# First attention of a two-block kernel: meta scores in one matmul per tile, norms of two units at once, five probability buffers and one unit more of lag

## What is computed

```python
def gqa_block(q_blk, k, v):
    s = jnp.einsum('bkgqd,bksd->bkgqs', q_blk, k).astype(jnp.float32) * (HEAD_DIM ** -0.5)
    p = jax.nn.softmax(s, axis=-1)
    return jnp.einsum('bkgqs,bksd->bkgqd', p.astype(v.dtype), v)
...
        a_out = attention_branch(q, k, v, q_g, k_g, cos, sin, n_tok) * jax.nn.silu(a_gate)
        mixed = jnp.concatenate([f_out, a_out], axis=-1)
        h = h + jnp.einsum('ble,ed->bld', mixed, w_out[i])
```

## Time and profile before

| | |
|---|---|
| median of 3 runs | 2139.82 us (2139.18 to 2145.11) |
| profiled execution | 2138.93 us, span of the instructions 2137.1 us |
| TensorE matmuls | busy 1979.6 us (93%) |
| TensorE weight loads | 1627.8 us (76%) |
| VectorE | 1333.7 us (62%) |
| ScalarE | 917.1 us (43%) |
| GpSimd | 929.2 us (43%) |
| mean granted TensorE clock | 0.973 |
| first attention | scores of unit 0 start at 307.4 us, last values matmul at 545.7 us |

### The profile page before, as it was taken

One profiled execution on the slowest core, in us unless ns is written; L12 is line 12 of the kernel. 1 busy time (PEld: TensorE's weight loads), 2 busy tenths in 40 slices (PEclk: granted clock), 3 DMA queues, 4 the chain that ended last, 5 costly groups with the idle time before them and its releaser, 6 DMA issues.

```text
span 2137.1 us, 25608 instructions
## 1 busy us (share of the span) xinstructions
PE 1979.6 (93%) x9543; PEld 1627.8 (76%) x9543; DVE 1333.7 (62%) x1860; ACT 917.1 (43%) x1614; POOL 929.2 (43%) x651
## 2 busy tenths in 40 slices
PE   5999999999999999997998798889999999999888
PEld 5987767777787888876777686767888887777776
DVE  5354058988786354455566546777655568868846
ACT  4112127878442223235666544543333343435541
POOL 0333308988000000005665100589999996746030
PEclk9999999999999999998999999999999999999999
DMA  3112100000323111100000221323232338676212
GB/s 149 50 40 90 50 0 1 1 1 1 138 91 137 48 40 40 40 22 30 21 20 21 107 90 60 138 89 119 89 109 81 117 108 307 226 264 209 79 40 99
DMA packets 68412, 179.57 MB, mean 84 GB/s; under 512 B 6529, under 2 KB 8321, under 8 KB 68289
## 3 DMA queue, kind: packets, MB, share of 16 engines
q1 hardware_dynamic: 44928, 124.39, 17.4%
q10 hardware_dynamic: 23360, 53.54, 7.0%
HBM read 148.02 MB, written 29.88 MB: 83 GB/s over the span
## 4 chain that ended last, share of the span: by engine, by line
PE 63%; DVE 15%; POOL 8%; issue 7%; ACT 5%; DMA 1%; ACTq 0%; SPq 0%; DVEq 0%; POOLq 0%
PE psb L341 14%; PE psa L341 12%; PE psc L2472 4%; PE psa L2472 4%; POOL wrf L2334 4%; PE psd L2472 3%; PE psb L2472 3%; PE psd L989 2%; PE psd L1925 2%; POOL wrl L2352 2%; PE psc L967 2%; PE psd L341 1%; DVE ltl L1909 1%; DVE wl L370 1%; PE psc L341 1%
## 5 line engine op out<-in xcount | busy, mean ns | idle before, releaser
L2334 POOL TENSOR_TENSOR wrf<-wr 128x512 f32<-128x512 f32 x155 | 250.2, 1618 | 245.2 <-DMA wr<-slabs 237.6
L1877 POOL TENSOR_TENSOR lps<-lps,tiny 128x128 f32<-128x128 f32 (+2 forms) x24 | 14.7, 615 | 454.6 <-DVE tiny L1872 452.0
L2347 ACT ACTIVATE wrh<-wrf 128x512 fp32r<-128x512 f32 x155 | 97.7, 630 | 180.0 <-POOL wrf L2334 178.0
L2352 POOL TENSOR_TENSOR wrl<-wrf,wrh 128x512 fp32r<-128x512 f32 x111 | 168.3, 1523 | 8.4 <-ACT wrh L2347 8.3
L1128 POOL TENSOR_TENSOR pb<-pb,tiny 128x1024 f32<-128x1024 f32 x64 | 121.3, 1896 | 79.0 <-DVE tiny L1087 77.4
L341 PE MATMUL psb<-mh,wh 128*128 128x512 f32 x352 | 125.0, 399 | 4.1 <-issue 2.4
L364 ACT ACTIVATE wh<-wraw 128x1024 fp32r<-128x1024 f32 x82 | 86.2, 1053 | 87.2 <-PE psb L341 45.9
L341 PE MATMUL psb<-ml,wh 128*128 128x512 f32 x352 | 123.1, 394 | 0.0
L341 PE MATMUL psb<-mh,wl 128*128 128x512 f32 x352 | 122.7, 393 | 0.0
L370 DVE TENSOR_TENSOR wl<-wraw,wh 128x1024 fp32r<-128x1024 f32 x75 | 92.1, 1231 | 35.3 <-ACT wh L364 31.4
L2352 POOL TENSOR_TENSOR wrl<-wr,wrh 128x512 fp32r<-128x512 f32 x62 | 106.7, 1724 | 16.3 <-ACT wrh L2347 15.9
(11 more groups left out here) (641 smaller groups left out, 5937.8 us busy)
## 6 DMA issues: line engine op xcount, KB each, us to landing
wraw<-slabs SPq DMA_DIRECT2D x98, 512.0 KB, 3.5
wr<-slabs SPq DMA_DIRECT2D x132, 256.0 KB, 4.6
wr<-slabs SPq DMA_DIRECT2D x40, 512.0 KB, 3.5
hidden<-hf ACTq DMA_DIRECT2D x22, 512.0 KB, 3.5
half_sums<-hsum ACTq DMA_DIRECT2D x22, 256.0 KB, 3.6
x<-xT SPq DMA_DIRECT2D x8, 520.0 KB, 9.5
h<-xT SPq DMA_DIRECT2D x8, 512.0 KB, 7.2
residual<-h ACTq DMA_DIRECT2D x8, 512.0 KB, 6.1
```

Of the source, the lines that this page charges most:

```text
L2334: e.tensor_tensor(WRF[n % NW][:, :], x, y, WEIGHTS[product(n)][2]).then_inc(*pooled.up(("sum", n)))
L2347: e.activation(WRH[n % NW][:, :], x, ACT.Copy).then_inc(*acted.up(("high part", n)))
L2352: e.tensor_tensor(WRL[n % NW][:, :], x, WRH[n % NW][:, :], SUB).then_inc(*pooled.up(("low", n)))
```

## The change

Five things, all in the first attention:

- The two parts of the keys lie in one tile KEYS, so one matmul per tile of queries reads the 16 meta columns of both parts, 32 columns. The two products lie side by side in PSUM. ScalarE copies the high one, and VectorE adds the low one to it (`dve_meta_scores`) before the maxima.
- The norms are made for two units at once, in every second step. The factor of 2 leaves the norm; a half is applied to the output instead, as a scale in ScalarE's copy and in VectorE's scalar-tensor-tensor.
- There are five probability buffers; exp of unit u waits for the transposes of unit u - 5.
- Transposes and their parts run 4 units behind the scores (LAG1), the values 8 (AHEAD).
- GpSimd's counter for the product of a unit is raised ahead of the meta product, which gets a counter of its own; the norms wait for that of an earlier unit.

```diff
-        KHH = [at(f"khh{j}", [P, L], F32R, 137.5 + 8.25 * j) for j in range(2)]
-        KLL = [at(f"kll{j}", [P, L], F32R, 141.625 + 8.25 * j) for j in range(2)]
+        KEYS = [at(f"keys{j}", [P, 2, 1056], F32R, 137.5 + 8.25 * j) for j in range(2)]
+        KHH = [k[:, 0, 0:L] for k in KEYS]
+        KLL = [k[:, 1, 0:L] for k in KEYS]
...
-        PB = [at(f"pb{j}", [P, T], F32, (154.75, 158.75, 112.75, 116.75)[j]) for j in range(4)]
+        PB = [at(f"pb{j}", [P, T], F32, (154.75, 158.75, 112.75, 116.75, 107.25)[j]) for j in range(5)]
...
-        LAG, AHEAD = 3, 7
+        LAG = 3
+        LAG1, AHEAD = 4, 8
...
-                o = PS[Dp][:, 0, v * META:v * META + META]
-                e.matmul(o, lhsT=QST[s][:, c0:c0 + P], rhs=KHH[s][:, T:L], start=True, stop=False,
-                         skip_group_check=True)
-                t = e.matmul(o, lhsT=QST[s][:, c0:c0 + P], rhs=KLL[s][:, T:L], start=False, stop=True,
+                t = e.matmul(PS[Dp][:, 0, 2 * v * META:2 * v * META + 2 * META].rearrange("p (a b) -> p a b", b=META),
+                             lhsT=QST[s][:, c0:c0 + P], rhs=KEYS[s][:, :, T:L], start=True, stop=True,
                              skip_group_check=True)
...
-                if 0 <= u - LAG < NU:
-                    pe_turns(e, u - LAG)
+                if 0 <= u - LAG1 < NU:
+                    pe_turns(e, u - LAG1)
...
-            if u >= 4:
-                e.wait_ge(*psum.on(("turned", u - 4, 1)))
-            e.activation(PB[v][:, :], both(u % 2), ACT.Exp, scale=scale1, bias=NB[:, v:v + 1],
+            if u >= 5:
+                e.wait_ge(*psum.on(("turned", u - 5, 1)))
+            e.activation(PB[u % 5][:, :], both(u % 2), ACT.Exp, scale=scale1, bias=NB[:, v:v + 1],
...
-        def dve_meta_max(e, g):
-            e.wait_ge(*acted.on(("meta s", g)))
-            e.tensor_reduce(MXT[:, 4 * (g % 2):4 * (g % 2) + 4], SMC[:, g % 2, :].rearrange("p (a b) -> p a b", b=META),
-                            AX.X, MAX).then_inc(*vec.up(("meta max", g)))
+        def dve_meta_scores(e, g):
+
+            e.wait_ge(*acted.on(("meta s high", g)))
+            e.tensor_tensor(meta_scores(g), meta_scores(g), meta_product(1), ADD).then_inc(*vec.up(("meta s", g)))
+            e.wait_ge(*vec.on(("meta s", g)))
+            e.tensor_reduce(MXT[:, 4 * (g % 2):4 * (g % 2) + 4], meta_scores(g), AX.X, MAX).then_inc(*vec.up(("meta max", g)))
...
-        def dve_norms(e, u):
-            v = u % 4
-            e.wait_ge(*acted.on(("exps", u)))
-            e.tensor_scalar(RI[:, v:v + 1], RSA[:, v:v + 1], RSM[:, v:v + 1], 2.0, ADD, MUL
-                            ).then_inc(*vec.up(("all sum", u)))
+        def dve_norms(e, u, n):
+
+            v = slice(u % 4, u % 4 + n)
+            e.wait_ge(*acted.on(("exps", u + n - 1)))
+            if u >= 4:
+                e.wait_ge(*pooled.on(("meta p", u + n - 5)))
+            e.tensor_tensor(RI[:, v], RSA[:, v], RSM[:, v], ADD).then_inc(*vec.up(("all sum", u)))
             e.wait_ge(*vec.on(("all sum", u)))
-            e.reciprocal(RI[:, v:v + 1], RI[:, v:v + 1]).then_inc(*vec.up(("one over", u)))
+            e.reciprocal(RI[:, v], RI[:, v]).then_inc(*vec.up(("one over", u + n - 1)))
...
-                if 0 < u - 1 < NU:
-                    dve_norms(e, u - 1)
+                if u == 2:
+                    dve_norms(e, 1, 1)
+                elif u > 2 and u % 2 == 0 and u <= NU:
+                    dve_norms(e, u - 2, 2)
...
-            e.tensor_tensor(OT[g % 2][mine, :], OT[g % 2][mine, :], PS[Dp][mine, 1, :], ADD
-                            ).then_inc(*vec.up(("out", g)))
+            e.scalar_tensor_tensor(out=OT[g % 2][mine, :], in0=PS[Dp][mine, 1, :], scalar=0.5, in1=OT[g % 2][mine, :],
+                                   op0=MUL, op1=ADD).then_inc(*vec.up(("out", g)))
```

More of the change, by code:

```diff
@@ L770, in fourier_free @@
             elif n == 7:
-                e.wait_ge(*acted.on(("meta s", 0)))
+                e.wait_ge(*vec.on(("meta s", 0)))
             elif n >= 2:
@@ L850, in dve_fourier @@
                 if n == 4:
-                    dve_meta_max(e, 0)
+                    dve_meta_scores(e, 0)
         def dve_four(e, n):
@@ L966, in pe_turns @@
                     c = (4 * h + kt) * P
-                    t = e.transpose(PS[C][:, h, kt * P:kt * P + P], PB[u % 4][:, c:c + P], SQC[:, 0, :])
+                    t = e.transpose(PS[C][:, h, kt * P:kt * P + P], PB[u % 5][:, c:c + P], SQC[:, 0, :])
                 t.then_inc(*psum.up(("turned", u, h)))
@@ L971, in pe_meta_turn @@
             e.wait_ge(*pooled.on(("meta parts", g)))
-            e.wait_ge(*acted.on(("meta s", min(g + 2, NG - 1))))
+            e.wait_ge(*vec.on(("meta s", min(g + 2, NG - 1))))
             for x in range(4):
@@ L1028, in act_parts, with meta_product, meta_scores @@
                              ).then_inc(*acted.up(("p high", u, h)))
+        def meta_product(part):
+            return PS[Dp][:, 0, 0:8 * META].rearrange("p (v a b) -> p v a b", a=2, b=META)[:, :, part, :]
+        def meta_scores(g):
+            return SMC[:, g % 2, :].rearrange("p (a b) -> p a b", b=META)
         def act_meta_scores(e, g):
@@ L1033, in act_meta_scores @@
                 e.wait_ge(*vec.on(("meta max", g - 2)))
-            e.activation(SMC[:, g % 2, :], PS[Dp][:, 0, 0:4 * META], ACT.Copy).then_inc(*acted.up(("meta s", g)))
+            e.activation(meta_scores(g), meta_product(0), ACT.Copy).then_inc(*acted.up(("meta s high", g)))
         def act_attention(e):
@@ L1038, in act_attention @@
                 g, phase = divmod(u - AHEAD, 4)
-                if 0 <= u - LAG < NU:
-                    act_parts(e, u - LAG)
+                if 0 <= u - LAG1 < NU:
+                    act_parts(e, u - LAG1)
                 if u < NU:
@@ L1057, in act_attention @@
                         e.wait_ge(*pooled.on(("gated", g - 2)))
-                    e.activation(OT[g % 2][mine, :], PS[Dp][rest, 1, :], ACT.Copy).then_inc(*acted.up(("out low", g)))
+                    e.activation(OT[g % 2][mine, :], PS[Dp][rest, 1, :], ACT.Copy, scale=0.5).then_inc(*acted.up(("out low", g)))
                 if u % 4 == 2 and u < NU - 4:
@@ L1117, in dve_attention @@
                 if u % 4 == 3 and u < NU - 4:
-                    dve_meta_max(e, u // 4 + 1)
-                if 0 <= u - LAG < NU:
-                    dve_parts(e, u - LAG)
+                    dve_meta_scores(e, u // 4 + 1)
+                if 0 <= u - LAG1 < NU:
+                    dve_parts(e, u - LAG1)
         def pool_attention(e):
@@ L1126, in pool_attention @@
                 if u < NU:
-                    e.wait_ge(*vec.on(("one over", u)))
-                    e.tensor_tensor(PB[v][:, :], PB[v][:, :], RI[:, v:v + 1].to_broadcast([P, T]), MUL)
+                    e.wait_ge(*vec.on(("one over", u if u < 2 else u // 2 * 2 + 1)))
+                    e.tensor_tensor(PB[u % 5][:, :], PB[u % 5][:, :], RI[:, v:v + 1].to_broadcast([P, T]), MUL
+                                    ).then_inc(*pooled.up(("p", u)))
                     e.tensor_tensor(PM[g % 2][:, v, :], PM[g % 2][:, v, :], RI[:, v:v + 1].to_broadcast([P, META]), MUL
-                                    ).then_inc(*pooled.up(("p", u)))
+                                    ).then_inc(*pooled.up(("meta p", u)))
                 if u < NU and v == 3:
@@ L1143, in pool_meta_parts @@
                 e.wait_ge(*psum.on(("meta turned", g - 2)))
-            e.wait_ge(*pooled.on(("p", 4 * g + 3)))
+            e.wait_ge(*pooled.on(("meta p", 4 * g + 3)))
             hi = PMS[g % 2][:, :, 0:META]
```

6 lines of the change are left out of this document (3 added, 3 removed).

## The result

The changed kernel takes 2146.37 us (median of 20 runs, 2141.84 to 2153.11), the kernel before 2139.65 (20 runs, 2134.23 to 2145.14). The ratio is 1.0034, with a 95% interval of 1.0026 to 1.0042: slower, by about the least that can be told apart. The time lies in the range on record, but 6 us above the forecast and not in the case held likeliest, no change, which had 0.76; slower had 0.11.

The account below looks back on a forecast made before the run. The prediction took a chain over ScalarE and VectorE to the output, plus GpSimd waits, to bound TensorE's loop. Terms 5.5 + 0.4 - 4.6 - 0.3 - 0.4 = +0.6 us gave 2140.4 us, range 2132 to 2147.

Parts of the forecast that it names:

- The meta matmuls at the new place: Loop, ahead of the light step: four meta matmuls lose their cover, +0.42 us per group, +5.5 us over 13 groups.
- GpSimd's waits: Loop: the lag makes GpSimd's products 2.2 us early, so all TensorE waits on GpSimd go, -4.6 us.
- The VectorE part: Loop, chain to the output: norm pair -0.04 us and output +0.07, together +0.03 per group, +0.4 us.
- The output: VectorE's output addition as scalar-tensor-tensor: 745 ns against 0.66 to 0.69 us, +0.07 us.
- The fill: First steps without values: scores start earlier, first light step at 345.2 instead of 345.54, -0.3 us.
- The tail: Last light step to output projection: last norms made together, last output ready at 14.6 us, -0.4 us.
- The clock falls: Rival: two waits in a group's light stretch lower TensorE's clock, 2148 us from four groups; 0.11 with dearer meta matmuls.
- TensorE's work is the bound: Rival: groups of 12.4 us by TensorE's issues alone, 2122 us; 0.13 together with a much shorter chain.
- GpSimd waits stay: Rival: pairs delay products by the lag's gain, so 2.2 us of waits and the clock's 2.4 stay, 2145 at most; 0.08.

Follow-up runs that it names:

- the lag alone: Kernel before with only turns 4 and values 8 units behind, five buffers and a wait of the norms for an earlier product: 2146.91 us, ratio 1.0039.
- staging later: Changed kernel with GpSimd's staging of the high queries one step later, behind the product of the group's third unit: 2155.29 us, ratio 1.0076.
- two-input norms: Kernel before with only each unit's norm addition reading two tensors, the factor of two moved to the output: 2154.17 us, ratio 1.0067.
- the output first alone: Kernel before with only the output's copy ahead of the exponentials (ScalarE) and its addition ahead of the maxima (VectorE): 2139.96 us, ratio 1.0006.
- one-input norms: Changed kernel with the norm addition as two instructions, each reading one tensor and a per-partition scalar: 2140.20 us, ratio 1.0004.
- the last experiment: Kernel before with only the output's copy ahead of the exponentials and its addition ahead of the maxima: 2139.96 us, ratio 1.0006.
- the one before it: Kernel before with meta scores in one matmul per tile, output copy ahead of the exponentials and output addition ahead of the maxima: 2136.37 us, ratio 0.9991.
- eight meta matmuls: Changed kernel with scalar-operand norms and meta scores in two matmuls of 16 columns per tile again: 2152.92 us, ratio 1.0066.
- output before bias: Changed kernel with scalar-operand norms and VectorE's output addition right behind the maxima, ahead of bias and norms: 2134.27 us, ratio 0.9985.
- output first: Changed kernel with scalar-operand norms, output copy ahead of the exponentials and output addition ahead of the maxima: 2132.75 us, ratio 0.9971.

## Why the prediction came out as it did

**The meta matmuls at the new place**, held. Four in 0.46 us (403.69 to 404.15) against 0.42; the difference of 0.44 us per group between eight and four was shown by the runs. The Trainium skill's figure weighed there (page "TensorE: Matmul & The Clock Gate", section "Back-to-back issue gap": about 81 ns for 128 columns) lost to the rows again: eight matmuls of 16 columns took 0.91 us, 0.11 each.

**GpSimd's waits**, held. No transpose waits for GpSimd in the loop of the changed kernel, nor in that of the lag alone. The short-and-long pattern is gone where no meeting falls: 13.78 and 13.93 us, within 0.03 of the sum.

**The VectorE part is the step that failed.** "Together +0.03 per group" rests on 162 ns for an addition of two tensors with 4 columns. That row ran where GpSimd was idle, and at such places the new addition is as short as was taken, 0.15 us. In the loop GpSimd is busy in four fifths of the time, and the form changed from one tensor with a per-partition operand, which ran at 0.20 to 0.22 us everywhere, to two tensors, both in SBUF. Five times in 13 groups it took 1.17 to 1.19 us on the chain: 5.2 us, and 1.5 for the clock that fell after one of these waits. The loop was forecast 1.3 us longer than before and came out 7.16 longer. Of the 5.9 between, 6.7 are these two; the last group, which has no meta scores ahead of it, was 0.5 shorter than I had taken it (13.32), and the others 0.03 each, which makes up the difference. The trace of before had the sign, had I looked for the same form beside GpSimd's work in other stages:

```profile
L2551 DVE TENSOR_TENSOR hsum<-hf x22: 678/1774/1779, 1418.9 to 1781.5; 128x512 f32<-128x512 f32 x22
```

Min, median and max again: this addition of two SBUF tiles of 512 columns takes 678 ns at best and 1774 in most cases. Twenty of the 22 began while a GpSimd instruction ran, and each ended 0.55 us after it; the two that began with GpSimd idle are the short ones. The Trainium skill, page "SBUF — State Buffer", section "SBUF: two separate sides", says that VectorE and GpSimd share a pair of ports as an exclusive lock, held for a whole instruction, and that on VectorE's side operations with two SBUF inputs take part in it, against a GpSimd operation that reads SBUF. By that rule an addition that comes while a GpSimd instruction runs ends just after it; the trace agrees: the ten long additions here, and the 26 over 0.5 us of two experiments (staging later, two-input norms), each end within 0.03 us after a GpSimd instruction that had begun before them. I should have weighed that rule; it was the one that spoke against this change.

**The output** as a scalar-tensor-tensor was priced at +0.07 and costs nothing: 677 ns in the mean against 0.66 to 0.69 before.

**The fill** was forecast at -0.3 and came out at +0.56, or at +1.2 counted from the scores of unit 0, which stood 0.67 us earlier (306.76 against 307.43). The first steps were quicker than I had them, but the meta scores, now ahead of the light step, wait for staging, which I hadn't looked at, and behind that wait the granted clock was 0.52 from 332.13 to 335.50 us, mostly the lower level:

```profile
331.66 0.62 PE L941 MATMUL psd<-keys,qst 128*128 128x32 f32 x4 [2.09 <-POOL qst L926]
```

**The tail** held: -0.44 for -0.4.

**The rivals.** "The clock falls" came true once in the loop, not from the cause I named (two short waits) but after a single one of 1.90 us. "TensorE's work is the bound" was not reached even where the output was ready in time: 13.4 us, not 12.4, since the exponentials come next. "GpSimd waits stay" did not happen. The mechanism that decided, a VectorE instruction held up by GpSimd, was none of them. That 2146.37 us still lies inside 2132 to 2147 is luck: the upper end was set for meta matmuls at more of their full duration and for a falling clock, not for this.

## What to carry to other kernels

Before an operation on VectorE gets a second operand in SBUF, look at what GpSimd does at that moment: a per-partition scalar operand or an operand in PSUM keeps it out of GpSimd's way, and one more instruction of 0.2 us can be cheaper than one that sometimes lasts 1.2. Take the price of an instruction from rows with the same operand kinds and the same neighbours, and look at its longest, not at its mean. When a wait is removed from a loop with two late engines, move the other one's work as well: the lag alone cost 0.39%, the output first alone gave nothing, and both together, with the meta scores in one matmul and one-input norms, gave 0.29% over the kernel before, some of which may be drift.

## What the runs showed of the hardware

- A VectorE addition of one or two numbers per partition, both operands in SBUF, takes 0.15 us alone and up to 1.69 us beside a GpSimd tensor-tensor, of any of three kinds (staging, product, gate); it ends within 0.03 us after it. A tensor-scalar with a per-partition operand (0.20 to 0.22 us), a reciprocal and an addition with one operand in PSUM run beside the same GpSimd instructions at their usual length.
- Where the two begin almost together, the GpSimd instruction can be the one that gets longer. In the kernel before with two-input norms, four additions began 0.02 to 0.03 us after the short GpSimd instruction for the low part of the meta probabilities and took 0.15 us, while that instruction took 0.36 us instead of 0.32; a fifth began 0.035 us after it and took 0.30 us.
- The granted clock fell in one or two groups of the loop in the kernels with longer waits of TensorE there: after 1.40 us in the kernel before, 1.90 in the changed one, 1.25 and 1.83 in the last experiment, 2.22 in the one before it. Waits as long or longer (2.48) also passed at 1.00. In the five kernels whose longest wait in the loop was 0.36 to 1.07 us (one-input norms, eight meta matmuls, lag alone, output before bias, output first) it fell in no group.
- One kernel run on two occasions differed by 0.19% in its ratio to the kernel before, with the same loop to 0.01 us; of the 6.0 us between the two profiled executions 2.8 stood ahead of the first attention.
